# A one-core decoder layer in fp32: first norm taken token by token, modulation groups and weight units in another order

## What is computed

```python
mod = (silu(c) @ ada_w + ada_b)                 # 9 vectors of 2048 for the prompt and each of 8 samples
h = _rmsnorm(x, g1) * (1 + sc1) + sh1
x = x + 0.5 * gt1 * _swiglu(h, f1g, f1u, f1d)   # (silu(h @ wg) * (h @ wu)) @ wd
h = _rmsnorm(x, g2) * (1 + sc2) + sh2
...                                             # RG-LRU heads beside window attention, then w_out
x = x + gt2 * (jnp.concatenate([lru_out, attn_out], axis=-1) @ w_out)
h = _rmsnorm(x, g3) * (1 + sc3) + sh3
x = x + 0.5 * gt3 * _swiglu(h, f2g, f2u, f2d)
```

## Time and profile before

| | |
|---|---|
| median of 3 runs | 2438.74 us (2437.61 to 2439.52) |
| the profiled execution | 2440.04 us, span 2438.2 us |
| PE busy | 2367.3 us (97%) |
| DVE busy | 1203.9 us (49%) |
| ACT busy | 878.9 us (36%) |
| POOL busy | 167.2 us (7%) |
| moved by DMA | 480.89 MB, mean 197 GB/s |
| mean granted TensorE clock | 0.988 |

### The profile page before, as it was taken

The page is one execution under the profiler, slowest core; times in us unless marked ns, Lnnn a source line. Parts: engine busy times, 40 slices in busy tenths (PEclk is TensorE's granted clock), DMA queues, the critical chain, the costliest instruction groups (busy, mean ns, idle before and its releaser), DMA issues.

```text
span 2438.2 us, 45800 instructions
## 1 busy us (share of the span) xinstructions
PE 2367.3 (97%) x17250; PEld 2262.3 (93%) x17250; DVE 1203.9 (49%) x2072; ACT 878.9 (36%) x1175; POOL 167.2 (7%) x195
## 2 busy tenths in 40 slices
PE   7999899999999999998999897999999999999998
PEld 3888899999999999997999897999999999999997
DVE  3565334434533454357676646354454454455444
ACT  3232222223222232234466634333333333333234
POOL 3000000000000000023031212000000000000002
PEclk9999999999999999999999998999999999999999
DMA  9999988888899858863444453554554554554552
GB/s 322 355 331 349 307 250 255 258 256 256 257 268 275 266 148 249 254 186 110 138 135 120 122 151 94 152 156 138 154 155 139 151 156 140 150 155 144 150 152 86
DMA packets 688437, 480.89 MB, mean 197 GB/s; under 512 B 15349, under 2 KB 611977, under 8 KB 687993
## 3 DMA queue, kind: packets, MB, share of 16 engines
q1 hardware_dynamic: 686416, 473.36, 64.9%
q0 software_dynamic: 1776, 6.26, 0.8%
q10 hardware_dynamic: 162, 0.14, 0.0%
HBM read 476.53 MB, written 5.13 MB: 198 GB/s over the span
## 4 chain that ended last, share of the span: by engine, by line
PE 91%; DVE 4%; ACT 2%; DMA 2%; issue 1%; POOL 0%; SPq 0%; DVEq 0%; POOLq 0%; ACTq 0%
PE ps L519 28%; PE ps L521 28%; PE ps L520 28%; PE ps L530 5%; PE ps L505 1%; DMA raw<-in_ffn_w_gate 1%; DMA mod_raw<-in_ada_w 1%; DVE h_lo L1279 1%; DVE lo L1233 1%; DVE work L1268 0%; PE ps L835 0%; ACT hi L913 0%; DVE work L1515 0%; PE ps L565 0%; PE ps L814 0%
## 5 line engine op out<-in xcount | busy, mean ns | idle before, releaser
L519 PE MATMUL ps<-h_hi,hi 128*128 128x320 f32 x3456 | 1082.7, 313 | 31.8 <-DVE lo L1233 15.3
L521 PE MATMUL ps<-h_hi,lo 128*128 128x320 f32 x3456 | 1072.8, 310 | 0.0
L520 PE MATMUL ps<-h_lo,hi 128*128 128x320 f32 x3456 | 1072.7, 310 | 0.0
L1233 DVE TENSOR_TENSOR lo<-raw,hi 128x1024 fp32r<-128x1024 f32 (+1 forms) x608 | 729.4, 1218 | 501.2 <-ACT hi L913 498.1
L913 ACT ACTIVATE hi<-raw 128x1024 fp32r<-128x1024 f32 (+1 forms) x608 | 623.7, 1049 | 945.2 <-PE ps L521 842.6
L519 PEld LDWEIGHTS ps<-h_hi,hi 128*128 128x128 f32 x3456 | 653.3, 189 | 51.6 <-issue 29.9
L520 PEld LDWEIGHTS ps<-h_lo,hi 128*128 128x128 f32 x3456 | 653.6, 189 | 0.2
L521 PEld LDWEIGHTS ps<-h_hi,lo 128*128 128x128 f32 x3456 | 653.2, 189 | 0.0
L519 PE MATMUL ps<-a_hi,hi 128*128 128x320 f32 x1376 | 426.8, 310 | 1.3 <-DVE a_lo L1387 1.3
L521 PE MATMUL ps<-a_hi,lo 128*128 128x320 f32 x1376 | 425.2, 309 | 0.0
L520 PE MATMUL ps<-a_lo,hi 128*128 128x320 f32 x1376 | 425.1, 309 | 0.0
(11 more groups left out here) (206 smaller groups left out, 912.2 us busy)
## 6 DMA issues: line engine op xcount, KB each, us to landing
raw<-in_ffn_w_gate SPq DMA_DIRECT2D x172, 512.0 KB, 4.1
raw<-in_ffn_w_up SPq DMA_DIRECT2D x172, 512.0 KB, 5.1
raw<-in_ffn_w_down SPq DMA_DIRECT2D x160, 512.0 KB, 4.8
mod_raw<-in_ada_w SPq DMA_DIRECT2D x144, 512.0 KB, 8.0
work<-in_ada_w SPq DMA_DIRECT2D x144, 512.0 KB, 8.2
raw<-in_w_in SPq DMA_DIRECT2D x56, 512.0 KB, 3.8
raw<-in_w_out SPq DMA_DIRECT2D x32, 512.0 KB, 3.8
raw<-in_ffn_w_down SPq DMA_DIRECT2D x16, 384.0 KB, 3.0
```

Of the source, the lines that this page charges most:

```text
L519: mm(out, w_hi, r_hi, start=first, stop=False)
L520: mm(out, w_hi, r_lo, start=False, stop=False)
L521: return mm(out, w_lo, r_hi, start=False, stop=last)
L1233: v.tensor_tensor(lo_slot(u)[:, 0:n], raw_slot(u)[:, 0:n], hi_slot(u)[:, 0:n], ALU.subtract).then_inc(lo_done, 1)
```

## The change

The first norm no longer goes through POOL and a matmul of ones over squared blocks: ACT squares the token rows of x with a running sum (three instructions), takes rstd per token with Ln and Exp, DVE scales three copies of the identity by it, and PE spreads it over all partitions by three matmuls of ones with these diagonals. x is turned one block for each modulation unit over units 0 to 13. DVE splits weight unit 0 behind the first modulate. In quarter 0 group 2 is used ahead of units 2 and 4 and group 3 ahead of units 5 and 6, and SP loads the parts in that order among the units. Group 12 goes out of the first down stage; it and all later groups stand one place on: chunks 1 to 3 use 12 to 29, the tail 30 and 31, the last chunk's up pairs 32 to 35. The counts of squares, sums and norms that follow shift by one.

```diff
-SUM_AT = MODS + 1
-SET_UP = 2
+TURN_AT = 2
+EARLY = ((2, 0, 2), (2, 4, 4), (3, 0, 5), (3, 4, 6))
+SET_UP = 3
...
-                def tail(u):
+                def tail(u, group):
                     for s in range(TAIL):
...
                             u += 1
+                            if group is not None and s > 0:
+                                mod_load((s - 1) * 4 + n, group + 1, group + 1)
                     for n in range(KB // 2):
...
                         u += 1
+                        if group is not None:
+                            mod_load(n, group + 2, group + 2)
                     return u
...
                     with sp.Fori(1, 4) as c:
-                        chunk(u0, c * 12, c, c * 6 + 7, True, True)
-                    u = tail(u0 + 4 * CH_U)
-                    with sp.Fori(0, 4) as i:
-                        up_pair(u, i * 2, 4 * CB * P + i * (2 * P), i + 31)
+                        chunk(u0, c * 12, c, c * 6 + 6, True, True)
+                    u = tail(u0 + 4 * CH_U, 30)
+                    with sp.Fori(0, 3) as i:
+                        up_pair(u, i * 2, 4 * CB * P + i * (2 * P), i + 32)
+                    up_pair(u + 3 * 8, 0, 4 * CB * P + 3 * 2 * P, None)
                     u += CB * 4
...
                         chunk(u0, c * 12, c, 0, False, False)
-                    chunk(tail(u0 + 4 * CH_U), 0, 4, 0, False, False)
+                    chunk(tail(u0 + 4 * CH_U, None), 0, 4, 0, False, False)
...
             head_group(1, range(MODS))
-            for u in range(4):
+            for u in range(8):
+                for group, first, at in EARLY:
+                    if u == at:
+                        head_group(group, range(first, first + 4))
                 head_unit(u)
-            head_group(2, range(MODS))
-            for u in range(4, 8):
+            for h in range(16):
+                head_group(4 + h // 2, range(h % 2 * 4, h % 2 * 4 + 4))
+                head_unit(8 + 2 * h)
+                head_unit(8 + 2 * h + 1)
+            for u in range(40, 46):
                 head_unit(u)
-            for q in range(QUARTERS):
-                u = 8 * q + 8
-                for i, (group, first) in enumerate(((3, 0), (3, 4), (4, 0), (4, 4))):
-                    head_group(2 * q + group, range(first, first + 4))
-                    head_unit(u + 2 * i)
-                    head_unit(u + 2 * i + 1)
-            for i, (group, first) in enumerate(((11, 0), (11, 4), (12, 0), (12, 4))):
-                head_group(group, range(first, first + 4))
-                head_unit(40 + 2 * i)
-                head_unit(40 + 2 * i + 1)
-            head_group(13, range(MODS))
+            head_group(12, range(4))
+            for u in range(46, 48):
+                head_unit(u)
+            head_group(12, range(4, MODS))
...
             def sum_of_squares(n):
-                pe.wait_ge(summed, n * KB + KB)
+                pe.wait_ge(summed, n * KB)
                 mm(psum[:, B_NORM, 0:T], ones, sum_sq, start=True, stop=True).then_inc(ms_ready, 1)
...
+            def spread_rstd():
+                pe.wait_ge(diag_ready, 1)
+                for t in range(3):
+                    n = P if t < 2 else SAMP
+                    last = mm(psum[:, 5, t * P:t * P + n], ones[0:n, :], diag[0:n, t, 0:n], start=True, stop=True)
+                last.then_inc(rstd_spread, 1)
+
             pe.wait_ge(x_in, 3 * 16)
+            for k in range(TURN_AT):
+                turn_x(k)
+            pe.wait_ge(c_ready, 1)
             for u in range(FIRST):
-                if u < MODS:
-                    turn_x(2 * u)
-                    turn_x(2 * u + 1)
-                if u == 0:
-                    pe.wait_ge(c_ready, 1)
                 mod_unit(u % MODS, u // MODS)
-                if u == MODS - 1:
+                if u + TURN_AT < KB:
+                    turn_x(u + TURN_AT)
+                if u == MODS - 2:
                     turn_parameters()
+                if u == MODS:
                     pe.wait_ge(prm_ready, 1)
                     mod_turn(0)
-                if u == SUM_AT:
-                    sum_of_squares(0)
+                if u == MODS + 1:
+                    spread_rstd()
             mod_turn(1)
...
                 for i in range(8):
-                    if i % 2 == 0:
+                    if q == 0:
+                        halves = [(group, part) for group, part, at in EARLY if at == i]
+                    else:
+                        halves = [(first if i < 4 else second, i % 4 * 2)] if i % 2 == 0 else []
+                    for group, part in halves:
                         for n in range(4):
-                            mod_unit(i % 4 * 2 + n, first if i < 4 else second)
+                            mod_unit(part + n, group)
                     quarter_unit(q, i)
-                    if i == 2:
+                    if i == (4 if q == 0 else 2):
                         mod_turn(first)
...
                         u += 1
+                    if group is not None:
+                        mod_turn(group + 1)
                     return u, g
...
                     down_with_groups(u0 + CB * 4, G_D0, (10, 11))
-                    down_with_groups(u0 + CB * 4 + 8, G_D0 + 8, (12,))
+                    down_with_groups(u0 + CB * 4 + 8, G_D0 + 8, ())
                     with pe.Fori(1, 4) as c:
-                        chunk(u0, c * 12, g0, c * 8, c * CB + a0, c * 6 + 7, True, True)
-                    u, g = tail(u0 + 4 * CH_U, g0 + 4 * CH_G)
+                        chunk(u0, c * 12, g0, c * 8, c * CB + a0, c * 6 + 6, True, True)
+                    u, g = tail(u0 + 4 * CH_U, g0 + 4 * CH_G, 30)
                     with pe.Fori(0, 4) as i:
-                        up_pair(u, i * 2, g, i, i + 31)
+                        up_pair(u, i * 2, g, i, i + 32)
                     u, g = u + CB * 4, g + 2 * CB
-                    down_eight(u, 0, g, 0, a0 + 4 * CB + TAIL, 35)
+                    down_eight(u, 0, g, 0, a0 + 4 * CB + TAIL, None)
                     down_eight(u, 2, g, 2, a0 + 4 * CB + TAIL, None)
...
                         chunk(u0, c * 12, g0, c * 8, c * CB + a0, 0, False, False)
-                    u, g = tail(u0 + 4 * CH_U, g0 + 4 * CH_G)
+                    u, g = tail(u0 + 4 * CH_U, g0 + 4 * CH_G, None)
                     chunk(u, 0, g, 0, a0 + 4 * CB + TAIL, 0, False, False)
...
+            act.dma_start(ident[:, :], io['identity']).then_inc(ident_in, 16)
             act.dma_start(c_tok[0:1, :], io['c_prompt']).then_inc(c_in, 16)
             act.dma_start(c_tok[1:NC_, :], io['c_sample']).then_inc(c_in, 16)
-            act.dma_start(ident[:, :], io['identity']).then_inc(ident_in, 16)
             act.wait_ge(c_in, 32)
...
                 act.wait_ge(ready, count)
-                if n * KB + m >= 2:
-                    act.wait_ge(summed, n * KB + m - 1)
+                at = (n - 1) * KB + m
+                if at >= 2:
+                    act.wait_ge(summed, at - 1)
                 run(sq[:, m % 2, :], x[:, m, :], ACT.Square).then_inc(squared, 1)
...
                 run(warm, eps, ACT.Ln)
-                act.wait_ge(ms_ready, n + 1)
+                act.wait_ge(ms_ready, n)
                 chain(run(ln_ms, psum[:, B_NORM, 0:T], ACT.Ln, bias=eps, scale=1.0 / D))
...
-            for k in range(KB):
-                square(k, 0, dve_freed, k + 1)
+            act.wait_ge(x_in, 3 * 16)
+            squares = h_hi[:, :, :].rearrange("p k n -> p (k n)")
+            more = h_lo[:, :, :].rearrange("p k n -> p (k n)")
+            for t in range(2):
+                run(squares[:, t * D:(t + 1) * D], x_tok[:, t, :], ACT.Square, accum_out=ssq[:, t:t + 1])
+            chain(run(more[0:SAMP, 0:D], x_tok[0:SAMP, 2, :], ACT.Square, accum_out=ssq[0:SAMP, 2:3]))
+            chain(run(ssq, ssq, ACT.Ln, bias=eps, scale=1.0 / D))
+            run(ssq, ssq, ACT.Exp, scale=-0.5).then_inc(tok_rstd, 1)
             copy_group(0)
+            act.wait_ge(rstd_spread, 1)
+            run(rstd, psum[:, 5, 0:T], ACT.Copy).then_inc(rstd_ready, 1)
+            copy_group(1)
             split(0)
-            run(warm, eps, ACT.Ln)
-            act.wait_ge(ms_ready, 1)
-            chain(run(ln_ms, psum[:, B_NORM, 0:T], ACT.Ln, bias=eps, scale=1.0 / D))
-            copy_group(1)
-            run(rstd, ln_ms, ACT.Exp, scale=-0.5).then_inc(rstd_ready, 1)
             modulate(0, 0, 0, Q)
...
                     u = 8 * q + i
-                    if i == 2:
+                    if i == (4 if q == 0 else 2):
                         copy_group(2 * q + 2)
...
                 v.tensor_copy(x[:, k, :], bank(k)).then_inc(dve_freed, 1)
-            parameters()
-            add_mod(0, 0)
-            split(0)
+                if k == 7:
+                    parameters()
+                if k == 9:
+                    add_mod(0, 0)
+                    dve.wait_ge(tok_rstd, 1)
```

(39 more changed lines are left out.)

65 lines of the change are left out of this document (40 added, 25 removed).

## The result

| | before | after |
|---|---|---|
| median | 2439.13 us, 4 runs (2437.61 to 2441.07) | 2469.20 us, 4 runs (2463.98 to 2471.78) |
| ratio, 95% interval | | 1.0122 [1.0111, 1.0134] |
| span of the profiled execution | 2438.2 us | 2469.9 us |

What follows compares the result with a forecast made beforehand. PE was taken as the bound, busy 2367.3 of 2438.2 us, leaving its idleness and lower-clock time to change. 3.0 + 12.7 + 3.0 - 11.8 + 2.0 + 8.3 = 17.2 us, giving 2456; range 2440 to 2466.

Steps and rivals of the forecast that it cites:

- part 1's "nothing" for ACT's squares: Head: ACT's three squares of a token row, about 1.91 us each, are ready long before needed and cost nothing.
- Part 1, the head: Up to the first product: modulation units among transposes run cold and unit 0's split comes later; +3.0 us, bounds -6 to +4.
- the clock rises in the head: Rival, chance 0.20: denser matmuls raise PE's clock in the head; first product near 46, 9 us less, 2447.
- Part 2, quarter 0: First quarter: weight loads queue on SP behind modulation parts that PE gates, so PE stalls; +12.7 us, bounds +5 to +16.
- Part 3, later boundaries: Units 18, 26 and 34 land late and ACT's splits delay the next stage; about 1.0 three times, +3.0 us, bounds 0 to 5.
- what is late next in part 4: Chunk 1's first pair: unit 55 arrives late behind SP's and POOL's loads; +2.0 us, bounds 0 and 6.
- Part 4, the hole: Group 12 leaves the first down stage: the 9.16 us wait and 2.6 of cold products go; -11.8 + 2.0 us.
- the hole at 272 stays: Rival, chance 0.12: POOL's 4.27 MB move into chunk 1 and starve units 52 to 55; part 4 nil, +9.8, 2466.
- Part 5, the tail: Tail with groups 30 and 31: down loads wait behind group 32's gated part; stall 6.2 plus restart, +8.3 us, bounds 0 and 10.

Runs made afterwards that it cites:

- experiments 1: After with SP's old queue order in the first pass (units 4 to 7 ahead of group 3, later half groups one place later); 2445.44 us, 1.0026 of before.
- experiment 3: After with group 32's parts loaded behind the tail's fourth down unit instead of the first; 2472.11 us, 1.0133 of before.
- 2: After with POOL's loads spread over the use of seven groups instead of starting together; 2462.50 us, 1.0114 of before.
- 5: Kernel before with only the new first norm and one x block per modulation unit, group and load orders unchanged; 2436.27 us, 0.9999 of before.
- 10: After with the LRU constants computed behind unit 5 instead of unit 1; 2475.39 us, 1.0146 of before.
- 8: Kernel 4 with group 2's first half used ahead of unit 0 and unit 0 split ahead of group 1's work; 2429.02 us, 0.9962 of before.
- 9: Kernel before with POOL's loads spread, the new norm with one block a unit, and unit 0 split early; 2424.49 us, 0.9939 of before.
- 4: After with the edits of experiments 1, 2 and 3 together; 2429.57 us, 0.9966 of before.
- 6: Kernel before with POOL's loads spread over the use of groups 13 to 19, nothing else; 2426.67 us, 0.9957 of before.

## Why the forecast had the right sign and was 13 us short

**What bounds the kernel** was read rightly. New idleness of PE, with the restart behind each wait, is the loss, and none of the cheaper or dearer instructions of the norm shows in the time (part 1's "nothing" for ACT's squares: its first took 1.91 us at 13.56, as costed from the earlier trace rows).

**Part 1, the head: +3.0 forecast, -6.0 in the profiled execution.** The rival "the clock rises in the head", which I gave 0.20, came true there: the unit at 23.23 is at 2.4 GHz (0.64 us instead of 1.08) and S is 46.20, where that rival said near 46. In experiments 1 and 3, with after's order in the head, S is 56.69 and 57.24, where my forecast said 55.1. Both courses occur: of nine such traces four (after, 2, 5, 10) have the rise before 30 us, so 0.20 looks low by these few. What the forecast lacked is that one order of work can go either way; that the profiled execution took the early course is luck. The Trainium skill (TensorE: Matmul & The Clock Gate, Part 4: PE-mode transpose) says that a transpose does not count as activity that brings the full clock. The two-block heads agree (1.08 us a unit until the blocks end, near 38); the one-block heads agree in 1, 3, 8 and 9, and not in after, 2, 4, 5 and 10, where the units reach 2.4 GHz among the transposes.

**Part 2, quarter 0: +12.7 forecast, +16.3 measured.** The mechanism is as forecast, in each of its steps. The timelines of SP, ACT and DVE in after:

```profile
55.99 1.90 SPq L368 DMA_DIRECT2D mod_raw<-in_ada_w  x4
57.94 0.63 SPq L357 DMA_DIRECT2D raw<-in_ffn_w_up  x1
```

```profile
65.88 1.06 ACT L942 ACTIVATE hi<-raw 128x1024 fp32r<-128x1024 f32 x1 [9.75 <-DMA raw<-in_ffn_w_up]
```

```profile
67.06 0.17 DVE L1340 TENSOR_SCALAR small<-small 128x8 f32<-128x8 f32 x1 [8.66 <-ACT small L1015]
...
71.45 0.81 DVE L1382 COPY work<-ps 128x640 f32<-128x640 f32 x1
```

Unit 5 is landed 19.7 us after S (forecast 18.5), from there to unit 4's start are 6.6 us (6.7), and PE had wanted it at S + 20.1 (19.8). The three waits are 6.20, 2.95 and 1.92, forecast 5.4, 1.9 and 2.0: 11.1 against 9.3. With the 1.9 of group 2 and the restart ahead of unit 4 (20 products, 2.5 where I had taken 1.6) that makes 15.5; the last 0.8 of the 16.3 I did not assign.

**Part 3, later boundaries: +3.0 forecast, +14.0 measured. This is the step that failed**, and the largest error. I took 1.0 three times, from unit 18 landing 9.7 after PE's use of the half group ahead of it: the waits are 3.31, 2.13 and 3.20, 8.6 in all. Unit 18's load came later than forecast:

```profile
128.07 1.93 PE L538 MATMUL ps<-work,c_t 128*32 128x256 f32 x32
```

```profile
128.77 2.20 SPq L368 DMA_DIRECT2D work<-in_ada_w  x4
```

```profile
140.15 1.06 ACT L942 ACTIVATE hi<-raw 128x1024 fp32r<-128x1024 f32 x1 [7.50 <-DMA raw<-in_ffn_w_gate]
```

From PE's use of the half group to the landing are 12.0 us, not 9.7. The first part lands 3.8 us after its issue, as forecast (3.7); the other three and the load take 7.5 us, where I had put 5.5 at 386 GB/s. For units 26 and 34 it is 10.5 and 11.7 us, so the three landings are 5.1 us later than forecast in all. Why these transfers ran below the pace of the earlier trace rows is not shown. The second half of the error is the restart. After a short wait I had counted nothing. In this stretch 47 products of after start 0.27 us apart (behind these three waits and behind the one of 1.92 at its start), and none did before: 47 x 0.12 = 5.6, and 8.6 + 5.6 = 14.2, against the measured 14.0. My bound for the three together, 5, did not hold it, nor did the bound of 6 for what is late next in part 4 (below), and so the range did not.

**Part 4, the hole: -9.8 forecast, -1.9 measured.** The hole at 272 goes, and the rival "the hole at 272 stays", 0.12, has its way in chunk 1: 7.58 us and 2.1 of restart. What is late next costs 9.9 us (-11.8 + 9.9), where I took 2.0. The bytes that I counted were right: with the late half SP had four parts and four halves on the way, 4.2 MB, beside POOL's 4.27. But I gave them the whole pace of 386 GB/s, 24.8 us after PE's use of the group; the late half landed after 30.2, at 319.87. Between 289.65 and 319.87 the queues moved 9.65 MB at 319 GB/s, 5.34 MB of it SP's. SP was held as well: it issued the part at 295.75 for 9.2 us and the late half at 305.20 for 6.1, where an issue takes 0.4 otherwise. From 311.90 on it issued four more parts, whose transfers ran beside the late half's. An estimate from these numbers: 9.65 MB at 386 GB/s take 25.0 us, 27.8 with the 2.8 ahead, so of the 5.4 us too late about 3.0 are other bytes and 2.4 the lower pace. Experiments 2 and 6 confirm the cause from both sides.

**Part 5, the tail: +8.3 forecast, +9.1 measured.** The wait of 7.86 (0.64 before) stands behind the chain that was forecast, with its landings 1.7 us later; PE was ready at 929.61, that is 4.7 after 924.88, as worked out. Experiment 3 removes it.

**By the parts**, then: the head gave 9 us more than forecast, and parts 2, 3 and 4 cost 3.6, 11.0 and 7.9 more, the tail 0.8: 17.2 - 9.0 + 23.3 = 31.5. The head's gain hid more than a third of the error. By estimate, with the head of experiment 3 (S 11.0 us later) the profiled execution would have been some 11 us longer still. That is for this execution only: the other three runs of after are 1.7 to 7.8 us faster than it, and their heads are not known.
